# A hybrid decoder layer on eight cores: separate banks for norm sums, tile-by-tile closing, two score banks, block-diagonal q, and a decay-gate product in bf16 parts

## The chip, the cores and the metric

The program runs on the 8 cores of one Trainium2 chip. The batch has 8 sequences, and each core computes one of them alone: 2048 tokens by 1024 channels. The metric is the device time of the slowest core in microseconds (us). Each core has TensorE (PE, matrix products, with its weight loads shown as PEld), VectorE (DVE), ScalarE (ACT), GpSimd (POOL) and SyncE (SP). Here POOL and SP do hardly more than issue DMAs.

## The reference, cut to what matters

```python
h = h + 0.5 * swiglu(rmsnorm(h), wg, wu, wd)          # first feed-forward half, D_FF = 2816
u = rmsnorm(h); z = u @ w_in                           # one input projection, then split by columns
# mixer 1: latent attention, 8 heads, q and k of 64+32 (rope), v of 64, causal softmax
# mixer 2: gated linear attention, 4 heads, dk = 64, dv = 128, chunks:
log_a = log_sigmoid(a_lr @ w_a2 + b_a) / 16            # a_lr has 16 columns: the decay gate
bcum  = cumsum(log_a) inside a chunk
q_t, k_t = q * 64**-0.5 * exp(bcum), k * exp(-bcum)
o = tril(q_t k_t^T) v + q_t S                          # S: the state before the chunk
S = exp(b_last) * S + (k * exp(b_last - bcum))^T v
# mixer 3: cross-attention of 4 heads of 128 into 256 memory tokens
merged = sum of sigmoid(gate) * (o_i @ w_o_i) over the three mixers
h = h + merged @ w_out
h = h + 0.5 * swiglu(rmsnorm(h), ...)                  # second feed-forward half
out = rmsnorm(h)
```

## The kernel before, in words

**Tiles and stages.** A core's 2048 tokens are four tiles of 512, numbered 0 to 3, with channels on the partitions. A matmul is 128 by 128 weights against 512 columns of tokens unless something smaller is said. The program is written in this order: the opening (norms of tiles 0 to 2), the first feed-forward half of tiles 0, 1 and 2 together, that of tile 3 alone, the mixers of tiles 0 and 1, the second half of tile 0, the mixer of tile 2, the second half of tile 1, the mixer of tile 3, and the second half of tiles 2 and 3 together.

**A planner sets the order.** Each operation is recorded with its dependencies and a cost, and `schedule` (line 206's `dma` and the helpers record them) plays the program through once with those costs and writes down the order of each engine. The smaller the priority number, the earlier an operation is taken when several are ready. The priority is the place in the program plus `f.base`. The feed-forward halves of single tiles (tile 3's first, tile 0's and tile 1's second) get a base of a million and more, so they fill TensorE where the mixers leave it free; below they are called the filler. On the chip each engine then runs its list strictly in order and waits on semaphores.

**Banks.** The eight PSUM banks of 512 f32 columns are given out by kind, with a limit for each in `limits`: `s` for attention scores, `o` for an attention head's output, `q` and `m` for projections, `x` for cross-attention, `g` for the linear attention's output, `f` and `w` for the feed-forward halves (three or two tiles, one tile), `n` for norm sums. Banks of one kind are opened in the order in which the program asks for them: no bank of kind `f` opens before an earlier one of kind `f` has. The seven weight buffers (`ring`) work in the same manner.

**A feed-forward half** (`ffn`) goes through its 22 blocks of 128 hidden columns in five splits. In a split, `gate_up` makes 16 matmuls for a block and a tile, ScalarE a silu and VectorE a product into `aF` (or, for tile 2, into a part of `ntm`); then `down` makes one matmul for each block of the split and each of 8 output rows, and VectorE adds it to the tile's `hS`. In the last split `landed` follows each `down`: `Squares.take` lets ScalarE square the row, and a matmul with `ones` adds it up in a bank of the sums' own kind, which is asked for with the first square. From the full sum `rstd` makes the norm's factor by a logarithm and an exponential, and eight VectorE operations scale the rows to the next stage's input (`nM[0]` for the mixer of tile 0).

**A mixer** (`mixer_tile`) projects, norms, and makes keys and values for the tile; then come 8 heads of causal attention over all tiles so far (score matmul, exponential on ScalarE, matmul with the values). Between heads `fill(2)` sets units of the two other mixers: `u_v`, `u_gates`, `u_q`, `u_k`, `u_kt`, then alternately `u_chunk` (linear attention over 128 tokens) and `u_x` (a cross-attention head). The merge with its 24 gate projections and the output projection follow.

**Names in rows.** `mb,B` are score matmuls, `mb,va` those with the values, `mb,ones` and `fb,ones` norm sums, `aF,ring` and `ntm,ring` or `B,ring` feed-forward or projection matmuls by the operand that streams. `f1g`, `f2g`, `f2bg` and `wb` are weights in HBM. Lines 562, 573, 588, 595, 600, 606 and 612 are the helpers for matmuls, transposes, activations, tensor-tensor, scalar-tensor-tensor, tensor-scalar and copies. Two pairs of lines matter most:

```python
    sums = [Squares(M2, M1, "f") for _ in range(3)]
    limits = {"f": 8, "w": 4, "s": 3, "o": 1, "q": 2, "m": 6, "g": 1, "x": 2, "n": 2, ...
```

## Time and profile before

| what | value |
|---|---|
| time, median of 3 runs | 1682.48 us |
| the other runs | 1679.72 and 1876.37 us |
| the profiled execution's own time | 1687.72 us |
| its span on the slowest core (core 1) | 1686.6 us |
| spans of the eight cores | 1673.0 to 1686.6 us |
| mean granted TensorE clock of core 1 | 0.992 |
| TensorE, VectorE, ScalarE busy | 1628.0, 872.0, 730.4 us |

The median is of whole runs; the rows are of one profiled execution, whose span is 1.1 us below its own time. A matmul counts as busy for its whole pipelined length, so the busy share of TensorE overstates the work in it. The run of 1876.37 us stands far from the other two, and nothing below rests on it.

### The profile page before, as it was taken

How to read it: one execution, taken by the hardware profiler on the slowest of the kernel's cores; microseconds unless marked ns; L12 is line 12 of the kernel's file. 1: busy time of each engine (PE TensorE's matmuls, PEld its weight loads, DVE VectorE, ACT ScalarE, POOL GpSimd, SP SyncE). 2: the span in 40 equal slices, each digit the busy share in tenths (PEclk: the TensorE clock that was granted, in tenths of full speed). 3: DMA queues.
4: the chain of work that ended last, by engine and by line, in shares of the span. 5: the costliest groups of instructions: out<-in, count | busy, mean ns of one | idle time of the engine just before them, and what ended most of it. 6: DMA issues, size and time to landing. Idle time of an engine off the chain costs nothing.

```text
span 1686.6 us, 24322 instructions; the slowest of 8 cores (1673.0 to 1686.6 us)
## 1 busy us (share of the span) xinstructions
PE 1628.0 (97%) x7859; PEld 753.9 (45%) x7859; DVE 872.0 (52%) x1490; ACT 730.4 (43%) x1182; POOL 120.6 (7%) x228
## 2 busy tenths in 40 slices
PE   6999999998999999999999999999999999999997
PEld 2445444434444444444444444454444444444443
DVE  6662442435765566654565644645645464433336
ACT  5213001046872256952477862268993221210114
POOL 0102011100000000000000000000000011001000
PEclk9999999999999999999999999999999999999999
DMA  9779999898566575555998774886464455623212
GB/s 212 106 114 124 139 125 110 129 148 208 104 146 157 151 154 111 111 130 167 252 207 181 159 192 151 256 220 154 133 192 129 159 157 157 178 70 100 76 38 100
DMA packets 80425, 249.10 MB, mean 148 GB/s; under 512 B 9440, under 2 KB 13808, under 8 KB 79856
## 3 DMA queue, kind: packets, MB, share of 16 engines
q0 software_dynamic: 28864, 107.49, 38.2%
q1 hardware_dynamic: 51440, 140.06, 26.9%
q8 instruction: 68, 1.11, 0.3%
q14 instruction: 53, 0.43, 0.1%
HBM read 282.91 MB, written 54.00 MB: 200 GB/s over the span
## 4 chain that ended last, share of the span: by engine, by line
PE 89%; DMA 4%; DVE 3%; ACT 3%; issue 2%; POOL 0%; DVEq 0%; ACTq 0%; SPq 0%; POOLq 0%
PE ps_all L562 88%; DMA ring<-f1g 2%; ACT mb L588 1%; DVE hS L600 1%; DMA ring<-wb 1%; ACT ma L588 1%; ACT L588 1%; DMA ring<-f2d 1%; DVE ntm L600 0%; DMA hS<-x 0%; DVE mb L595 0%; ACT fa L588 0%; DVE aF L595 0%; DVE gU L600 0%; ACT B L611 0%
## 5 line engine op out<-in xcount | busy, mean ns | idle before, releaser
L562 PE MATMUL ps_all<-ntm,ring 128*128 128x512 bf16 x2224 | 530.5, 381 | 5.1 <-ACT ma L588 2.2
L562 PE MATMUL ps_all<-B,ring 128*128 128x512 bf16 x2016 | 450.4, 379 | 2.8 <-DVE gU L600 1.0
L562 PEld LDWEIGHTS ps_all<-ntm,ring 128*128 128x128 bf16 x2224 | 216.3, 98 | 267.1 <-issue 21.1
L588 ACT ACTIVATE fa<-ps_all 128x512 f32<-128x512 f32 x170 | 101.4, 598 | 468.9 <-PE ps_all L562 460.5
L562 PEld LDWEIGHTS ps_all<-B,ring 128*128 128x128 bf16 x2016 | 195.9, 98 | 237.7 <-issue 8.3
L562 PE MATMUL ps_all<-aF,ring 128*128 128x512 bf16 (+1 forms) x1264 | 294.3, 375 | 3.7 <-DVE hS L600 1.7
L600 DVE SCALAR_TENSOR_TENSOR hS<-ps_all,hS 128x512 f32<-128x512 f32 (+1 forms) x256 | 170.0, 672 | 99.6 <-PE ps_all L562 98.4
L595 DVE TENSOR_TENSOR aF<-fa,ps_all 128x512 bf16<-128x512 f32 x148 | 101.3, 686 | 226.0 <-PE ps_all L562 219.6
L562 PEld LDWEIGHTS ps_all<-aF,ring 128*128 128x128 bf16 x1264 | 123.4, 98 | 147.5 <-issue 10.7
L588 ACT ACTIVATE mb<-ps_all 128x512 bf16<-128x512 f32 (+1 forms) x304 | 161.5, 576 | 39.0 <-PE ps_all L562 36.0
L588 ACT ACTIVATE ma<-ps_all,hv 128x512 f32<-128x512 f32 x104 | 71.2, 687 | 183.1 <-PE ps_all L562 162.2
L588 ACT ACT_TABLE_LOAD x85 | 109.1, 1283 | 42.9 <-PE ps_all L562 27.2
L600 DVE SCALAR_TENSOR_TENSOR ma<-ma,ps_all 128x512 f32<-128x512 f32 x96 | 65.8, 687 | 113.4 <-PE ps_all L562 106.5
L562 PE MATMUL ps_all<-mb,va 128*128 128x512 bf16 (+1 forms) x320 | 108.8, 347 | 0.9 <-DVE om L595 0.5
L562 PE MATMUL ps_all<-mb,B 128*128 128x512 bf16 (+2 forms) x320 | 96.3, 348 | 4.5 <-ACT mb L588 1.7
L562 PE MATMUL ps_all<-mb,ring 128*128 128x512 bf16 (+1 forms) x416 | 93.5, 374 | 1.1 <-ACT B L611 0.9
L600 DVE SCALAR_TENSOR_TENSOR fa<-fa,ps_all 128x512 f32<-128x512 f32 x66 | 45.2, 685 | 70.8 <-ACT fa L588 66.5
L588 ACT ACTIVATE ma<-ps_all 64x512 f32<-64x512 f32 (+2 forms) x96 | 57.0, 597 | 22.3 <-PE ps_all L562 20.5
L588 ACT ACTIVATE mb<-hS 128x512 bf16<-128x512 f32 (+1 forms) x72 | 40.7, 580 | 56.4 <-DVE hS L600 49.4
L588 ACT ACTIVATE ma<-ma 128x512 f32<-128x512 f32 (+2 forms) x102 | 62.1, 619 | 5.0 <-DVE ma L976 1.0
L562 PEld LDWEIGHTS ps_all<-mb,ring 128*128 128x128 bf16 x416 | 40.5, 98 | 46.5 <-issue 6.5
L562 PE MATMUL ps_all<-mb,ones 128*128 128x512 bf16 (+1 forms) x120 | 41.6, 375 | 19.4 <-ACT mb L588 18.6
(129 smaller groups left out, 1215.1 us busy)
## 6 DMA issues: line engine op xcount, KB each, us to landing
ring<-wb SPq DMA_DIRECT2D x112, 512.0 KB, 4.4
ring<-f1g POOLq DMA_DIRECT2D x44, 512.0 KB, 10.4
ring<-f2bg POOLq DMA_DIRECT2D x44, 512.0 KB, 3.6
wb<-wm POOLq DMA_DIRECT2D x28, 512.0 KB, 14.7
ma<-spill SPq DMA_DIRECT2D x48, 256.0 KB, 5.5
ring<-wb SPq DMA_DIRECT2D x48, 256.0 KB, 3.7
ring<-f2g POOLq DMA_DIRECT2D x22, 512.0 KB, 8.6
f2bg<-ring SPq DMA_DIRECT2D x22, 512.0 KB, 5.5
```

The lines of the kernel that those rows point to most:

```text
L562: i = e.matmul(_ap(o), lhsT=_ap(l), rhs=_ap(r), start=st, stop=sp)
L588: f.add([("act", lambda e: e.activation(out=_ap(out), in_=_ap(in_), func=func, scale=_ap(scale), **kw), c_act(out, bias is not None))], ou ...
L595: f.add([(eng, lambda e: e.tensor_tensor(out=_ap(out), in0=_ap(a), in1=_ap(b), op=op), c_dve(out, rate))], outs=[out], ins=[a, b, *extra_ins])
L600: f.add([("dve", lambda e: e.scalar_tensor_tensor(out=_ap(out), in0=_ap(in0), scalar=_ap(scalar), in1=_ap(in1), op0=op0, op1=op1), c_dve(o ...
```

## The change

It has five parts.

1. **Sums' own banks.** The norm sums at the end of the two joint feed-forward stages take banks of kind `n` instead of `f`.
2. **Tile-by-tile closing of the first half.** In the last split tile 1 does its gate and up products, its downs and its norm, then tile 0, then tile 2, each followed by `close1`: before, all gate and up products came first, then all downs. Tile 1's hidden values now stand in the part of `ntm` that tile 0's mixer input takes over, tile 2's in `aF`. The reload and norm of tile 3 follow the close of tile 1 and 0, at the ordinary priority. The eight weight conversions (`wb<-wm`) of this split are issued during tile 1's products. `rope_tables` of tiles 0 and 1 get a lower priority.
3. **Two score banks** instead of three (`"s": 2`).
4. **The gated mixer.** `u_q` writes q_t of a pair of heads as a block-diagonal matrix `qz` of 128 by 1024, so one score matmul of 256 columns serves two heads (two a chunk instead of four of 128), and the state is kept as 128 by 128 for a pair instead of 128 by 256 with a mask. The copies to `ktz` and the mask `blk` go. The state's update is four matmuls with 64 weight columns and 128 streamed columns, two of which write output partitions 64 to 127. The products with the state come before those with v and take 256 columns each. `u_v` splits its weights by rows of the contraction, so it makes 8 matmuls of 512 columns where it made 16 of 256.
5. **The decay gate's product.** `a_lr @ w_a2` was a matmul in f32 with 16 rows. Now both operands are cut into three bf16 parts, laid out along 128 rows so that one bf16 matmul adds seven of the part products. The weights are cut once in `late_constants` (eight VectorE operations on 128x256), the activations once in each mixer (four small operations on 32 partitions where there was one copy).

The planner's cost of an f32 matmul is also raised, with no f32 matmul left.

```diff
@@ limits
-    limits = {"f": 8, "w": 4, "s": 3, "o": 1, "q": 2, "m": 6, "g": 1, "x": 2, "n": 2,
-              "rf": 7, "rw": 3, "rm": 4}
+    limits = {"f": 8, "w": 4, "s": 2, "o": 1, "q": 2, "m": 6, "g": 1, "x": 2, "n": 2, "rf": 7, "rw": 3, "rm": 4}
@@ late_constants
-        f.dma("sp", wa2_t, wa2_d, nbytes=16384, after=f.last_pe)
+        w32 = M2.get()
+        f.dma("sp", w32[:, 0:256], wa2_d, nbytes=131072, after=f.last_pe)
...
+        part = M1.get()
+        for i in range(3):
+            cp(part[:, 0:256], w32[:, 0:256], eng="dve")
+            if i < 2:
+                tt(w32[:, 0:256], w32[:, 0:256], part[:, 0:256], ALU.subtract)
+            if i:
+                stt(wa2_t, part[:, 0:256], vecs[:, V_SEL + i:V_SEL + i + 1], wa2_t, ALU.mult, ALU.add)
+            else:
+                ts(wa2_t, part[:, 0:256], vecs[:, V_SEL:V_SEL + 1], None, ALU.mult)
@@ mixer_tile
-        cp(ga_t, pk[0:16, :])
+        rest = M2.get()
+        cp(ga_t[0:32, :], pk[0:32, :])
+        cp(ga_t[96:128, :], pk[0:32, :])
+        tt(rest[32:64, :], pk[32:64, :], ga_t[0:32, :], ALU.subtract)
+        cp(ga_t[32:64, :], rest[32:64, :])
+        tt(ga_t[64:96, :], rest[32:64, :], ga_t[32:64, :], ALU.subtract)
@@ u_q, u_k
-                stt(st["q"].bf()[:, pr * TT:(pr + 1) * TT], p, 0.125, st["E"][pr], ALU.mult, ALU.mult)
+                for o2 in range(2):
+                    rows = slice(64 * o2, 64 * o2 + 64)
+                    stt(qz[pr][rows, o2 * TT:(o2 + 1) * TT], p[rows, :], 0.125, st["E"][pr][rows, :], ALU.mult, ALU.mult)
...
-                for o2 in range(2):
-                    o = o2 * 64
-                    cp(ktz[pr * 2 + o2][o:o + 64, :], kb[o:o + 64, pr * TT:(pr + 1) * TT], eng="dve", rate=4.0)
@@ u_v
-                mm([(p[:, v * 256:(v + 1) * 256], nM[k][:, i * 128:(i + 1) * 128], st["wv"][v][:, k, :], k == 0, k == 7)
-                    for v in range(2) for k in range(8)])
+                mm([(p, nM[k][:, i * 128:(i + 1) * 128], st["wv"][k // 4][:, k % 4, :], k == 0, k == 7) for k in range(8)])
@@ u_chunk
-            mm([(pa[:, h4 * 128:(h4 + 1) * 128], ktz[h4][:, csl], q[h4 // 2], True, True) for h4 in range(4)])
+            mm([(pa[:, pr * 256:(pr + 1) * 256].re("p (h n) -> p h n", h=2), k[pr], q[pr], True, True) for pr in range(2)])
...
-            mm([(pd[:, pr * 256:(pr + 1) * 256], kt[:, pr * 128:(pr + 1) * 128], v[:, pr * 256:(pr + 1) * 256], True, True)
-                for pr in range(2)])
+            mm([(pd[h4 % 2 * 64:h4 % 2 * 64 + 64, h4 // 2 * 128:(h4 // 2 + 1) * 128], kt[:, h4 * 64:(h4 + 1) * 64],
+                 v[:, h4 * 128:(h4 + 1) * 128], True, True) for h4 in range(4)])
...
-            for h4 in range(4):
-                o = po[:, h4 * 128:(h4 + 1) * 128]
-                g.append((o, v[:, h4 * 128:(h4 + 1) * 128], am[:, h4 * 128:(h4 + 1) * 128], True, False))
-                g.append((o, gS[n % 2][h4 // 2][:, (h4 % 2) * 128:(h4 % 2 + 1) * 128], q[h4 // 2], False, True))
+            for pr in range(2):
+                g.append((po[:, pr * 256:(pr + 1) * 256].re("p (h n) -> p h n", h=2), gS[n % 2][pr], q[pr], True, False))
+                for h4 in (2 * pr, 2 * pr + 1):
+                    hsl = slice(h4 * 128, (h4 + 1) * 128)
+                    g.append((po[:, hsl], v[:, hsl], am[:, hsl], False, h4 % 2 == 1))
...
-                stt(gU[pr], gU[pr], gp, pd[:, pr * 256:(pr + 1) * 256], ALU.mult, ALU.add)
-                stt(gS[(n + 1) % 2][pr], gU[pr], gdec[par][pr][:, i:i + 1], blk, ALU.mult, ALU.mult)
+                stt(gU[pr], gU[pr], gp, pd[:, pr * 128:(pr + 1) * 128], ALU.mult, ALU.add)
+                ts(gS[(n + 1) % 2][pr], gU[pr], gdec[par][pr][:, i:i + 1], None, ALU.mult)
@@ the first half's stage
         if j in (2, 3):
+            f.base = LATER // 2
             rope_tables(j - 2)
+            f.base = 0
...
-    sums = [Squares(M2, M1, "f") for _ in range(3)]
-    ffn(f1_d, [nB[0], nB[1], nB[2]], (0, 1, 2), "f", True, lambda i, c: sums[i].take(hslot[i][c]), side1, by_tile=(1, 0, 2),
-        opening=OPENING)
-    take_over(NTB[2], aT[2])
-    keep_rstd(1, sums[1].rstd("f"), M2)
-    spill(1, 1)
-    r = sums[0].rstd("f")
-    for c in range(8):
-        scaled(nM[0][c], hslot[0][c], V_MIX, c, r)
-    M2.put(r)
-    keep_rstd(2, sums[2].rstd("f"), M2)
-    spill(2, 2)
-    take_over(NTB[0] + NTB[1], hslot[2])
...
     f.base = LATER
-    load_x(3, 1)
-    rmsnorm(hslot[1], [vcol(V_F1 + c) for c in range(8)], D, nB[3], banks="n", wide=F2, narrow=F1)
...
+    sums = [Squares(M2, M1, "n") for _ in range(3)]
+    def close1(i):
+        r = sums[i].rstd("f")
+        if i == 0:
+            for c in range(8):
+                scaled(nM[0][c], hslot[0][c], V_MIX, c, r)
+            M2.put(r)
+            rmsnorm(hslot[1], [vcol(V_F1 + c) for c in range(8)], D, nB[3], banks="n")
+            return
+        keep_rstd(i, r, M2)
+        spill(i, i)
+        if i == 2:
+            take_over(NTB[0] + NTB[1], hslot[2])
+            return
+        take_over(NTB[2], aT[2])
+        load_x(3, 1)
+    ffn(f1_d, [nB[0], nB[1], nB[2]], (0, 1, 2), "f", True, lambda i, c: sums[i].take(hslot[i][c]), side1,
+        by_tile=(1, 0, 2), opening=OPENING, closed=close1, acts=[aT[0], aT[2], aT[1]])
@@ the last stage
-    sums_l = [Squares(M2, M1, "f") for _ in range(2)]
+    sums_l = [Squares(M2, M1, "n") for _ in range(2)]
```

**How the order moves at the first half's close.** TensorE, last split: before, the last 188 gate and up matmuls of the three tiles, then tile 1's downs with their sums.

```order
L562 MATMUL ps_all<-B,ring 128x512 x188
L562 MATMUL ps_all<-aF,ring 128x512 x4
L562 MATMUL ps_all<-mb,ones 128x512
L562 MATMUL ps_all<-aF,ring 128x512 x18
L562 MATMUL ps_all<-mb,ones 128x512
L562 MATMUL ps_all<-aF,ring 128x512 x2
L562 MATMUL ps_all<-mb,ones 128x512
L562 MATMUL ps_all<-aF,ring 128x512 x3
```

After, the same place: tile 1's last gate and up products and its downs, and further on tile 2's last products and its downs.

```order
L560 MATMUL ps_all<-B,ring 128x512 x60
L560 MATMUL ps_all<-ntm,ring 128x512 x18
L560 MATMUL ps_all<-mb,ones 128x512
L560 MATMUL ps_all<-ntm,ring 128x512 x2
L560 MATMUL ps_all<-mb,ones 128x512
L560 MATMUL ps_all<-ntm,ring 128x512 x3
...
L560 MATMUL ps_all<-B,ring 128x512 x36
L560 MATMUL ps_all<-ntm,ring 128x512 x24
L560 MATMUL ps_all<-aF,ring 128x512 x18
L560 MATMUL ps_all<-mb,ones 128x512
L560 MATMUL ps_all<-aF,ring 128x512 x2
L560 MATMUL ps_all<-mb,ones 128x512
```

The sum no longer stands between the first four downs and the rest but behind 18 of them, and 24 projection matmuls of tile 0's mixer (`ntm,ring`) stand ahead of tile 2's downs.

**In the last stage,** TensorE, where tile 2 ends. Before:

```order
L562 MATMUL ps_all<-B,ring 128x512 x60
L562 MATMUL ps_all<-aF,ring 128x512 x4
L562 MATMUL ps_all<-mb,ones 128x512
L562 MATMUL ps_all<-aF,ring 128x512 x18
L562 MATMUL ps_all<-mb,ones 128x512
L562 MATMUL ps_all<-aF,ring 128x512 x2
L562 MATMUL ps_all<-mb,ones 128x512
```

After:

```order
L560 MATMUL ps_all<-B,ring 128x512 x60
L560 MATMUL ps_all<-aF,ring 128x512 x18
L560 MATMUL ps_all<-mb,ones 128x512
L560 MATMUL ps_all<-aF,ring 128x512 x2
L560 MATMUL ps_all<-mb,ones 128x512
L560 MATMUL ps_all<-aF,ring 128x512 x3
L560 MATMUL ps_all<-mb,ones 128x512
```

The first sum moves from behind 4 downs to behind 18.

**In the attention of tile 3,** TensorE, a stretch without projections. Before:

```order
L562 MATMUL ps_all<-mb,va 128x512
L562 MATMUL ps_all<-ntm,ring 128x512 x4
L562 MATMUL ps_all<-mb,va 128x512
L562 MATMUL ps_all<-mb,B 128x512 x2
L562 MATMUL ps_all<-mb,va 128x512
L562 MATMUL ps_all<-mb,B 128x512
L562 MATMUL ps_all<-ntm,ring 128x512 x4
```

After:

```order
L560 MATMUL ps_all<-mb,va 128x512
L560 MATMUL ps_all<-aF,ring 128x512 x7
L560 MATMUL ps_all<-mb,va 128x512
L560 MATMUL ps_all<-mb,B 128x512 x2
L560 MATMUL ps_all<-mb,va 128x512
L560 MATMUL ps_all<-aF,ring 128x512 x7
L560 MATMUL ps_all<-mb,va 128x512
L560 MATMUL ps_all<-mb,B 128x512 x2
```

A score stands in both wherever a bank comes free; after, six or seven filler matmuls stand between scores where there were four. Counted over the whole list in matmuls of 512 columns, the work from the first to the last score matmul of a tile is 270, 374, 510 and 618 before and 298, 422, 562 and 778 after, of 7367 in both. From tile 3's last score to the end there are 1871 before and 1541 after.

## Rows read from the trace of the kernel before

**Rows 1.** The page: span, busy time, the chain by engine.
```profile
span 1686.6 us, 24322 instructions; the slowest of 8 cores (1673.0 to 1686.6 us)
...
PE 1628.0 (97%) x7859; PEld 753.9 (45%) x7859; DVE 872.0 (52%) x1490; ACT 730.4 (43%) x1182; POOL 120.6 (7%) x228
...
PE 89%; DMA 4%; DVE 3%; ACT 3%; issue 2%; POOL 0%; DVEq 0%; ACTq 0%; SPq 0%; POOLq 0%
```

**Rows 2.** Stages: us, length, then busy us by engine, clock, DMA.
```profile
core 1: us, PE busy (x) PEld busy (x) DVE busy (x) ACT busy (x) POOL busy (x), PEclk, DMA share, GB/s
0.00:50.00 50.00, 37.20 (x146) 14.90 (x147) 33.73 (x76) 26.05 (x41) 4.13 (x11) 0.97 0.87 193
75.00:100.00 25.00, 22.93 (x104) 9.65 (x103) 21.82 (x40) 1.85 (x3) 3.12 (x6) 1.00 0.93 120
350.00:400.00 50.00, 41.82 (x172) 16.75 (x170) 23.47 (x35) 25.82 (x43) 2.60 (x5) 0.93 0.93 189
...
400.00:1285.00 885.00, 864.28 (x4317) 406.93 (x4316) 501.59 (x892) 547.35 (x881) 39.58 (x75) 1.00 0.66 165
1285.00:1630.00 345.00, 345.00 (x1601) 156.36 (x1599) 157.13 (x232) 63.92 (x98) 33.17 (x60) 1.00 0.40 125
1630.00:1687.00 57.00, 42.36 (x222) 21.66 (x220) 28.57 (x55) 22.29 (x40) 0.00 (x0) 0.90 0.20 74
```

**Rows 3.** TensorE by shape: busy us, mean ns of one | idle before.
```profile
L562 PE MATMUL ps_all<-ntm,ring 128*128 128x512 bf16 x2224 | 530.5, 381 | 5.1 <-ACT ma L588 2.2 <-DVE hS L600 1.1 <-DVE aF L595 0.4
...
L562 PE MATMUL ps_all<-cs 16*128 16x512 f32 x16 | 9.2, 653 | 0.0
```

**Rows 4.** TensorE's timeline in a mixer: start, length, what, [idle before].
```profile
421.36 1.12 PE L562 MATMUL ps_all<-cs 16*128 16x512 f32 x2
422.41 1.04 PE L562 MATMUL ps_all<-ring,mb 128*128 128x512 bf16 x4
...
441.87 0.22 PE L562 MATMUL ps_all<-ma,gS 128*128 128x128 bf16 x1
441.93 0.22 PE L562 MATMUL ps_all<-mb,ma 128*128 128x128 bf16 x1
```

**Rows 5.** TensorE's timeline where the first half closes.
```profile
359.26 0.38 PE L562 MATMUL ps_all<-mb,ones 128*128 128x512 bf16 x1 [1.67 <-ACT mb L588]
...
385.66 0.38 PE L562 MATMUL ps_all<-mb,ones 128*128 128x512 bf16 x1 [1.86 <-ACT mb L588]
...
393.21 0.58 PE L562 MATMUL ps_all<-fb,ones 128*128 128x512 bf16 x1 [0.71 <-ACT fb L588]
```

**Rows 6.** Timeline of TensorE under the rope tables.
```profile
92.27 1.24 PE L562 MATMUL ps_all<-ntm,ring 128*128 128x512 bf16 x5 [1.10 <-DVE hS L600]
93.97 1.24 PE L562 MATMUL ps_all<-aF,ring 128*128 128x512 bf16 x5 [0.46 <-DVE hS L600]
```

**Rows 7.** TensorE's timeline where tile 2 ends its last half.
```profile
1639.15 0.38 PE L562 MATMUL ps_all<-aF,ring 128*128 128x512 bf16 x1 [0.36 <-DVE aF L595]
1641.19 0.38 PE L562 MATMUL ps_all<-mb,ones 128*128 128x512 bf16 x1 [1.67 <-ACT mb L588]
1641.40 5.73 PE L562 MATMUL ps_all<-aF,ring 128*128 128x512 bf16 x18
```

**Rows 8.** DMA issues from 355 to 400 us: KB each, us to landing.
```profile
ring<-f1g POOLq DMA_DIRECT2D x3, 512.0 KB, 12.6
```

**Rows 9.** Longest waits of TensorE, 400 to 1285 us.
```profile
PE ps_all L562 <- ACT ma L588: 3.7, 5, 1.5
```

**Rows 10.** Attention of tiles 2 and 3, columns as in rows 2.
```profile
880.00:990.00 110.00, 108.49 (x563) 51.49 (x561) 59.10 (x117) 90.53 (x151) 7.39 (x14) 0.99 0.78 180
1130.00:1260.00 130.00, 125.59 (x639) 58.58 (x638) 71.65 (x136) 114.86 (x194) 7.48 (x15) 1.00 0.60 162
```

**Rows 11.** ScalarE from 1130 to 1260 us by shape.
```profile
L588 ACT ACTIVATE mb<-ps_all 128x512 bf16<-128x512 f32 x101 | 55.9, 599 | 7.7 <-PE ps_all L562 7.1
```

**Rows 12.** VectorE, 400 to 1285 us, the linear attention's state.
```profile
L600 DVE SCALAR_TENSOR_TENSOR gS<-gU,gd,blk_s 128x256 bf16<-128x256 f32 x32 | 15.4, 482 | 2.1
```

60 lines of the change are left out of this document (32 added, 28 removed).

## The prediction

> **What bounds the kernel now.** I read the page first, then the stages, then single stretches of TensorE's timeline. The page says that TensorE is busy 1628.0 of 1686.6 us and that 89% of the chain that ended last is its matmuls [rows 1]. So two things can shorten the program: fewer or cheaper matmuls, and fewer gaps between them. Busy time overstates the matmuls. One of 512 columns lasts 381 ns in the mean [rows 3], but in the stage without a gap 1601 of them fill 345.00 us [rows 2], 0.2155 us each. A matmul of 128 columns follows its forerunner after about 0.056 to 0.06 us [rows 4], so columns set the time and an instruction costs some 2.5 ns beside them. Priced so by width, the list of the program (6987 matmuls of 512 columns, 504 of 256, 64 of 384, 288 of 128, 8 in f32) is 1598 us of pure streaming. The other 88 us of the span are gaps and stretches at a lower clock.
>
> Where they lie, from the stages [rows 2], each length less its matmuls by width: 0 to 50 us has 146 matmuls, 31.5 us of work, so 18.5 us lost; 75 to 100 has 104, 22.4 us, so 2.6 lost; 350 to 400 has 172, 37.1 us, so 12.9 lost; 1285 to 1630 loses nothing; 1630 to 1687 loses 17.5, most of it the tail behind the last matmul. The 885 us of the mixers hold what is left, about 34 us.
>
> **Part 1, the f32 product.** One f32 matmul (two records) starts at 421.36 and the next instruction at 422.41 [rows 4], 1.05 us; by the group it is 9.2 / 8 = 1.15 us [rows 3]. I take 1.10. In bf16 with 128 rows it is 0.216. Eight of them: 8 x (1.10 - 0.22) = 7.1 us off TensorE, all on its path. The other changed matmuls keep their columns: scores 4 x 128 become 2 x 256, `u_v` 16 x 256 become 8 x 512, state and output 1024 columns in fewer pieces. That is 160 instructions less in all, 0.3 to 0.4 us. Together **-7.4**. The four small operations on the activations a tile and the eight on the weights lie on VectorE and ScalarE, busy 872 and 730 of 1687 us [rows 1]; against them stand the `ktz` copies that go and the state updates at half their width, of which one took 482 ns 32 times [rows 12]. I cost these at nothing; the cover is the filler, and without it the longer chain ahead of `u_gates` would show, some 2 us a tile.
>
> **Part 2, the 64-column matmuls.** The trace has none, so I bound them. Below: two that write different halves of the partitions might overlap, 32 x 0.056 = 1.8 us saved. Above: if TensorE emptied its pipeline whenever the weight shape changes, a change would cost 381 - 216 = 165 ns [rows 3], twice in each of 16 chunks, 5.3 us. I take 0, since no row shows TensorE waiting between shapes: around the f32 matmuls, a change of rows and type, the follower starts at its price. The Trainium skill (TensorEngine Tiling (Array Packing), section Tiling Modes, under Key Properties) says that changing the tiling mode drains TensorE, which speaks for the upper end; by it the sum below would be 18 instead of 23.
>
> **Part 3, the close of the first half.** Before, the first sum matmul stands behind four downs in the order, and all later banks of its kind wait with it: TensorE stood 1.67 us at 359.26, 1.86 at 385.66, then 0.71 and more while tile 3's squares came from ScalarE [rows 5]. The clock fell too, to 1.2 GHz for some microseconds after these waits: a mean of 0.93 over the 50 us is 3.5 us of the 12.9 [rows 2]. After, 18 downs stand ahead of the first sum, other tiles' products cover the closes of tiles 1 and 0, and 24 projections of tile 0's mixer cover tile 2's; tile 3's norm comes in between. I expect a quarter of the loss to stay. Its place is weights: tile 3's blocks and the mixer's weights are wanted within some 10 to 20 us of the buffers' release (45 to 90 matmuls later in the order), and a load took 12.6 us to land here [rows 8] at a DMA share of 0.93 [rows 2]. So **-9.7**. What is moved with it: eight conversions go to the POOL queue within 14 us instead of 41, but the down weights stand ahead of them in its list; behind them stand only tile 3's first blocks. The reload of tile 3 stands on SP's queue ahead of the projection weights and waits for the spill of tile 1, which has 55 us for it.
>
> **Part 4, rope tables.** TensorE waited 1.10 and 0.46 us, and shorter, for `hS` updates queued behind rope operations on VectorE [rows 6], 2.6 us in the stage [rows 2]. In the new order at most one rope operation stands between two updates, and the second table comes in a stretch of products. **-2.3**. The weights' cutting comes shortly before; there VectorE has some 2.8 us free of every 3.5, and eight operations of at most 0.48 us are 3.8 us. If its 128 KB land late, the eight banks cover about 8 us.
>
> **Part 5, the last stage.** At 1641.19 TensorE stood 1.67 us for the first square, and the 18 downs behind it took 5.73 us where 18 x 0.216 + 0.17 = 4.1 are due [rows 7]: after the wait some of them ran at the lower of the clock's two levels, 1.2 GHz instead of 2.4 (granted clock 0.90 over the stage [rows 2]). 1.7 + 0.2 + 1.6 + a little of the 0.36 before: **-3.7**. The rest of the tail has no change.
>
> **Part 6, two score banks.** A tile's 3 banks let TensorE run ahead of ScalarE by three scores, two banks by two. ScalarE is busy 90.53 of 110 us in tile 2's attention and 114.86 of 130 in tile 3's [rows 10], and an exponential takes 599 ns [rows 11]. With two banks it will wait oftener for a score, so attention lasts longer: in the order 62 us more over four tiles (298 + 422 + 562 + 778 less 270 + 374 + 510 + 618, by 0.216). TensorE does filler meanwhile, so this costs nothing while there is filler. Behind tile 3's last score stand 1541 matmuls; merge, output projection and the last stage need about 1460 (384 + 1056 and sums), so some 80 are filler, 17 us of cover, where some 410 were before. TensorE's own waits in the mixers are many and short, the longest sum 3.7 us in five waits [rows 9]. They come from lateness of single results, and I see reasons both ways: fewer scores ahead expose it more, a less crowded ScalarE and one more bank for the others less. **0**, with -17 to +12 for the range: half of the 34 us gone, or a third more.
>
> **The sum.** -7.4 - 9.7 - 2.3 - 3.7 = -23.1 us. The profiled execution took 1687.7 us, 1.1 above its span and 5.2 above the median of the runs. A difference of this size carries over as it is: 1682.5 - 23.1 = **1659 us**.
>
> **The rivals.**
> *The mixers' waits halve.* For it: the bank that the scores give up goes to filler and projections, and many of the 34 us are waits on ScalarE, saturated at 88% in tile 3's attention [rows 10]. Against: the largest waits are for other things, such as a first product after a norm. It gives 1659 - 17 = 1642.
> *The close keeps its loss.* Late weights bring back the 9.7 us, a wait on `ring` loads in place of the wait on squares [rows 8]: 1669.
> *Each chunk drains TensorE twice.* The mechanism of part 2: 1659 + 5 = 1664. The Trainium skill's sentence quoted there is the one ground for it beside the missing row; by the trace it is neither borne out nor excluded.
> *Slower: ScalarE starves and the filler runs out.* Place: attention of tile 3. Each of its 120 exponentials waits for a score which stands behind a projection of 8 matmuls, 1.7 us, or a filler group of 4; if on the chip that is 0.7 us more each than planned, it is 84 us, of which 17 are covered, and the time is 1659 + 67 = 1726. Slower by 2% is reached from 0.57 us each. Against: ScalarE's time is planned with the same order, and the stage's plan of before (618 x 0.216 = 133 us) matches its 130.
>
> **How the numbers follow.** Forecast 0.50, halved waits 0.22, the close keeps its loss 0.15, drains 0.08, slower 0.05. The forecast's own range is 1650 to 1668. The whole range, 1641 to 1674, takes in the rivals but the last and the bounds of part 2. A measurement of this kernel tells about 2% from no change, 1649 to 1716. The halved waits fall below it, and a small part of the forecast: 0.26 faster. Slower 0.05, the same 0.69.
>
> **What would show it.** Right: 512-column bf16 matmuls `wa2s,ga` of 0.216 us, no gap over 1 us between 340 and 400 us and no lower clock there, no wait before the first `mb,ones` 45 us from the end. Part 2: the matmul behind the `64x128` ones starting more than 0.1 us late. Part 6: attention of tile 3 over 160 us long with TensorE full, and filler behind it. Wrong: gaps on `ring` loads after the close, PE idle in the last attention with ScalarE waiting for PE in every `mb<-ps_all`, or mixers whose gaps sum to something else than 34 us.

## The result, and the profile after

The changed kernel takes 1661.27 us in the median of six runs (1656.58 to 1662.19), the kernel before, on the same chip, 1681.12. The ratio is 0.988 with a 95% interval of 0.9865 to 0.9894: 20 us less, inside what counts as no change by the 2% bound. Forecast were 1659 us and 23 us less. The sum holds; several of its terms do not, as the profile shows. In some executions of any of these kernels the cores of one die show a lower clock and take longer; the ratios here and below are of the other executions.

The page of the changed kernel, to be read beside [rows 1]:

```profile
span 1659.7 us, 23972 instructions; the slowest of 8 cores (1650.2 to 1659.7 us)
...
PE 1616.8 (97%) x7691; PEld 741.1 (45%) x7691; DVE 873.4 (53%) x1501; ACT 744.1 (45%) x1195; POOL 120.2 (7%) x227
...
PE 89%; DMA 5%; DVE 2%; ACT 2%; issue 1%; SPq 0%; DVEq 0%; ACTq 0%; POOLq 0%
```

TensorE still bounds the kernel, with 168 instructions fewer. Its stages, with the columns of [rows 2]:

```profile
core 7: us, PE busy (x) PEld busy (x) DVE busy (x) ACT busy (x) POOL busy (x), PEclk, DMA share, GB/s
75.00:100.00 25.00, 25.00 (x118) 11.35 (x116) 20.32 (x33) 0.60 (x1) 3.12 (x6) 1.00 0.91 123
350.00:400.00 50.00, 46.11 (x208) 20.39 (x207) 25.98 (x40) 32.33 (x50) 1.63 (x3) 0.97 0.60 165
400.00:1262.00 862.00, 848.76 (x4100) 388.77 (x4099) 490.83 (x871) 515.55 (x824) 45.97 (x87) 0.99 0.66 171
...
1604.00:1660.00 56.00, 42.99 (x227) 22.53 (x224) 28.59 (x55) 22.17 (x40) 0.00 (x0) 0.91 0.23 76
```

75 to 100 us has no gap left (118 matmuls instead of 104). 350 to 400 holds 208 matmuls instead of 172, but a gap of 3.9 us is in it. The last stage's clock is 0.91 where it was 0.90.

To compare kernels stage by stage I add up, from the start times of TensorE's matmuls, each one's distance to the next less its price: its columns at 2.4 GHz and 2.5 ns, and 1.10 us for an f32 product, the prediction's prices. The sum of the prices is called the streaming work; it is worked out from the list of matmuls, not measured. What remains is lost to gaps and to the lower clock. Stages are cut by work done, so that the same matmuls stand in each; the numbers are medians of the six cores whose records are complete. "Attentions" is from a tile's first score to its last, "projection" the 25 us ahead of each attention, in which the key/value projection lies. The times are ratios to the kernel before on the same chip, by its 1682 us.

```
kernel                          us off  opening side close attentions projection other  ffn2 start end
before                             0     18.3   2.8  11.1     21.5       5.2      3.3     0.0     15.8
after                            -20.2   18.2   0.0   6.5      7.3      12.6      3.4     1.2     15.5
```

"Side" is the stretch with the rope tables, "other" the rest of the mixers, "ffn2 start" the stretch behind the last attention. The streaming work fell from 1598.3 to 1590.9 us, and each line and its streaming work add up to its median core's span (1676.6 and 1656.2 us) within 0.6 us. So the 20 us are: 7.4 of streaming, 2.8 at the rope tables, 4.6 in the close, 14.2 in the attentions, less 7.4 given back in the projection and about 1 behind the last attention.

**The close.** SP's queue, ScalarE and TensorE on core 7 of the changed kernel, against [rows 5]:

```profile
357.06 0.33 SPq L206 DMA_DIRECT2D hS<-x  x1
358.30 2.71 ACT L586 ACTIVATE mb<-hS 128x512 bf16<-128x512 f32 x5 [4.52 <-DMA hS<-x]
359.59 1.01 PE L560 MATMUL ps_all<-mb,ones 128*128 128x512 bf16 x2 [3.89 <-ACT mb L586]
...
359.00:363.00 4.00, 3.41 (x9) 1.26 (x10) 0.69 (x1) 3.72 (x8) 0.00 (x0) 0.57 0.89 330
```

The many short waits are one long one. It is not for weights: ScalarE waits 4.52 us for the reload of tile 3's rows, because the squares of tile 3's norm stand ahead of tile 0's last squares in its list, and TensorE's sum needs the latter. On all eight cores this is TensorE's one long wait here, 3.3 to 5.6 us. The reload is late because it waits for the spill of tile 1 out of the same rows: its last two DMAs went out from 340.16 us on and took 15.8 us to land in the median, and the reload's first DMA went out only at 352.19. Behind the wait the granted clock is 0.57 over four microseconds, most of them at 1.2 GHz.

**The projection of keys and values**, tile 1, core 7; `ga` marks the cutting of the gate's input:

```profile
613.27 0.68 DVE L593 TENSOR_TENSOR ma<-ps_all,ga 32x512 f32<-32x512 f32 x1
613.89 0.59 PE L560 MATMUL ps_all<-mb,ring 128*128 128x512 bf16 x2
614.58 0.59 ACT L609 ACTIVATE B<-ps_all 64x512 bf16<-64x512 f32 x1 [1.56 <-PE ps_all L560]
615.20 0.63 ACT L609 ACTIVATE ga<-ma 32x512 bf16<-32x512 f32 x1
615.27 0.69 DVE L610 CAST B<-ps_all 64x512 bf16<-64x512 f32 x1 [0.60 <-ACT B L609]
616.11 0.59 PE L560 MATMUL ps_all<-mb,ring 128*128 128x512 bf16 x2 [1.63 <-DVE B L610]
616.45 0.68 DVE L593 TENSOR_TENSOR ga<-ma,ga 32x512 bf16<-32x512 f32 x1
618.22 1.51 PE L560 MATMUL ps_all<-mb,ring 128*128 128x512 bf16 x4 [1.52 <-ACT B L609]
620.62 1.01 PE L560 MATMUL ps_all<-ring,mb 128*128 128x512 bf16 x2 [0.89 <-DVE B L610]
```

Two matmuls, then a wait for the copies out of their bank, and again. The same stretch of core 1 before had two waits of 0.9 us. The cutting is five operations where there was one copy (two copies, a subtraction, a copy, a subtraction), not the four that the text ahead of the prediction and its part 1 count. Nothing in the prediction speaks of this place.

**The f32 product and the state's matmuls.** By shape, the whole of core 7's mixers:

```profile
L560 PE MATMUL ps_all<-ga,wa2s 128*128 128x512 bf16 x8 | 3.1, 386 | 0.0
L560 PE MATMUL ps_all<-ma 128*64 128x128 bf16 x64 | 4.8, 231 | 0.2 <-ACT ma L586 0.2
```

and the timeline around one of each:

```profile
418.23 0.38 PE L560 MATMUL ps_all<-ga,wa2s 128*128 128x512 bf16 x1
418.44 0.81 PE L560 MATMUL ps_all<-B,ring 128*128 128x512 bf16 x3
...
694.88 0.38 PE L560 MATMUL ps_all<-mb,va 128*128 128x512 bf16 x1
695.18 0.30 PE L560 MATMUL ps_all<-ma 128*64 128x128 bf16 x4
695.42 0.39 PE L560 MATMUL ps_all<-mb,va 128*128 128x512 bf16 x1
```

The gate's product is at 0.21 us what the prediction said. From 694.88 to 695.42 are 0.54 us for one matmul of 512 columns and four of 128 columns, by width 0.216 + 4 x 0.056 = 0.44: 0.10 us over in each of 16 chunks, 1.6 us. The four together last 0.30 us from the first start to the last end. Four that follow each other at 0.056 us would last 3 x 0.056 + 0.231 = 0.40, so some of them overlap, as the run on them below shows.

**The last stage**, against [rows 7]:

```profile
1633.66 1.89 PE L560 MATMUL ps_all<-B,ring 128*128 128x512 bf16 x8
1636.93 0.60 PE L560 MATMUL ps_all<-aF,ring 128*128 128x256 bf16 x4 [1.38 <-DVE aF L593]
1638.72 0.27 PE L560 MATMUL ps_all<-mb,ones 128*128 128x256 bf16 x1 [1.19 <-ACT mb L586]
1638.83 3.58 PE L560 MATMUL ps_all<-aF,ring 128*128 128x256 bf16 x18
...
1639.00:1643.00 4.00, 4.00 (x23) 2.96 (x22) 1.75 (x5) 1.64 (x4) 0.00 (x0) 0.57 0.00 0
```

The wait on tile 2's first square is gone. Behind the waits at the turn of tile 3, 1.38 and 1.19 us, the clock is now down (0.57 in the row), on all six cores with complete records, and the end costs 15.5 us instead of 15.8. Before, of the same six only core 1, the one of [rows 7], had it down behind its wait of 1.67 us, where 18 downs took 5.73 us. On the other five, here core 7, the same wait had no fall behind it:

```profile
1633.68 0.38 PE L562 MATMUL ps_all<-mb,ones 128*128 128x512 bf16 x1 [1.67 <-ACT mb L588]
1633.89 4.04 PE L562 MATMUL ps_all<-aF,ring 128*128 128x512 bf16 x18
```

### The profile page after: what moved, and what is told of

It is laid out like the page before. It is cut to its first block, busy times and chain, and to the rows that moved or that the text cites. A ratio compares the mean times of both kernels' runs of the same rounds, so it can differ in the third digit from the quotient of the medians.

```text
span 1659.7 us, 23972 instructions; the slowest of 8 cores (1650.2 to 1659.7 us)
## 1 busy us (share of the span) xinstructions
PE 1616.8 (97%) x7691; PEld 741.1 (45%) x7691; DVE 873.4 (53%) x1501; ACT 744.1 (45%) x1195; POOL 120.2 (7%) x227
## 4 chain that ended last, share of the span: by engine, by line
PE 89%; DMA 5%; DVE 2%; ACT 2%; issue 1%; SPq 0%; DVEq 0%; ACTq 0%; POOLq 0%
PE ps_all L560 89%; DMA spill<-hS 1%; DMA ring<-f1g 1%; DMA hS<-x 1%; DMA ring<-wb 1%; ACT L586 1%; DMA rstd<-ma 1%; ACT ma L586 0%; DVE hS L598 0%; ACT mb L586 0%; DVE B L598 0%; ACT fa L586 0%; DVE aF L593 0%; DVE ma L593 0%; ACT B L609 0%
## 5 line engine op out<-in xcount | busy, mean ns | idle before, releaser
L560 PE MATMUL ps_all<-aF,ring 128*128 128x512 bf16 (+1 forms) x1264 | 301.8, 378 | 4.3 <-ACT B L609 2.1
L586 ACT ACTIVATE mb<-ps_all 128x512 bf16<-128x512 f32 (+1 forms) x304 | 165.0, 573 | 74.7 <-PE ps_all L560 71.4
L586 ACT ACTIVATE mb<-hS 128x512 bf16<-128x512 f32 (+1 forms) x80 | 44.6, 583 | 58.1 <-DVE hS L598 46.5
```

What stands on the lines that cost most here:

```text
L560: i = e.matmul(_ap(o), lhsT=_ap(l), rhs=_ap(r), start=st, stop=sp)
L586: f.add([("act", lambda e: e.activation(out=_ap(out), in_=_ap(in_), func=func, scale=_ap(scale), **kw), c_act(out, bias is not None))], ou ...
```

## The experiments

Twelve kernels. Each "us off" is the ratio to the kernel before, times 1682 us, less 1682; the ratio's 95% interval is given at each run. All twelve in the account's columns, with the two kernels for comparison:

```
kernel                          us off  opening side close attentions projection other  ffn2 start end
before                             0     18.3   2.8  11.1     21.5       5.2      3.3     0.0     15.8
before, price +1 ns              +7.9    15.7   2.8  11.2     23.1       6.6      4.1     0.4     16.3
before, two score banks         -10.3    17.0   2.8  11.8      9.5       2.5      5.5     0.8     17.5
before, parts 3 to 5             -4.4    17.7   0.0   8.5     17.0       6.3      7.9     0.0     13.7
before, mixer's parts            +3.0    17.0   4.4  11.0     19.8      11.6      6.2     0.0     16.7
after                            -20.2   18.2   0.0   6.5      7.3      12.6      3.4     1.2     15.5
after, price +1 ns              -21.4    16.7   0.0   9.9      5.3      14.7      2.4     0.8     13.7
after, price -1 ns               -4.0    17.7   2.8   6.7     13.6       7.3      6.5     8.4     14.5
after, three score banks         +0.7    17.1   0.0   8.4     18.3      13.0      7.0     5.5     13.7
after, kv banks of kind m        -3.4    17.6   0.0   8.6     11.9      10.6     10.3     6.2     14.6
after, f32 product               -7.2    16.6   0.0   8.5      8.3       5.2      8.3     6.9     15.3
after, reload planned later     -26.7    18.0   0.0   2.0      7.3      12.2      5.5     1.2     13.5
... and cutting written later   -30.3    17.7   0.1   2.0      8.9       6.5      4.2     2.7     15.3
after, 64-column probe           +5.5    17.0   0.0   8.8     12.9      13.6      6.1     1.2     14.9
```

**Three score banks again.**

```
-    limits = {"f": 8, "w": 4, "s": 2, ...
+    limits = {"f": 8, "w": 4, "s": 3, ...
```

> The changed kernel with three score banks instead of two, nothing else. My theory: in the changed kernel the two banks lowered the gaps of TensorE in the four attentions (21.5 us of loss before, 6 to 9 after) and raised them in the key/value projection just ahead of each attention, which takes its banks from the same kind (some 4 us before, 12 to 15 after, half of it low clock behind the waits). With three banks I expect the attention lengths back near 65/88/115/142 us, the attention losses back to 15 to 22 us, the loss in the 22 us ahead of the attentions back to 4 to 6 us, so 0 to 8 us more in total than the changed kernel: about 1665. Rival A, that the better attention came from the other edits (fewer instructions of the gated mixer, cheaper state updates) and not from the banks: attention losses stay at 6 to 9 us while those ahead of it fall, about 1654. Rival B, that the banks do nothing to the time: 1661, with losses as in the changed kernel.

Ratio 1.0004 (0.9987 to 1.0022). The attentions lose 18.3 us instead of 7.3, as the theory said. The projection still loses 13.0, and its two long waits, here on core 3, are the changed kernel's 1.63 and 1.52 us:

```profile
614.00 0.59 PE L560 MATMUL ps_all<-mb,ring 128*128 128x512 bf16 x2 [1.63 <-DVE B L610]
616.11 1.86 PE L560 MATMUL ps_all<-mb,ring 128*128 128x512 bf16 x4 [1.52 <-ACT B L609]
```

So the number of score banks has nothing to do with that wait, and the half of my theory that blamed it falls. The run is 21 us slower than the changed kernel, more than the 11 us of the attentions: some 10 came up elsewhere, 4 of them in one gap behind the last attention.

**The projection's banks of another kind.**

```
         for j in range(4):
-            p = bank("s")
+            p = bank("m")
             proj(wkv, j * 128, 128, ckvn, p, nk=2)
```

and the same in the loop for the values.

> The changed kernel with the eight banks a tile of the key/value up-projection taken from the filler's kind (up to six banks) instead of the scores' kind (two), nothing else. My theory: TensorE's waits for copies out of two banks just before each attention (1.63, 1.52 and 0.89 us at tile 1's in the changed kernel) go, and with them the low clock behind them (6.83 us at half clock there, 3.4 us at tile 2's): the loss in the 22 us ahead of the four attentions falls from some 12 to 15 us to 2 to 5, attention unchanged, 1651 to 1655. Rival: the waits are for VectorE and ScalarE themselves, which are busy with the norms there, so any bank waits alike; then the loss stays within 2 us and the time is 1661.

Ratio 0.998 (0.9966 to 0.9993). The projection loses 10.6 us, hardly less, so it isn't short of banks of its kind; by the account 5 us more are lost in the attentions, 7 in the rest of the mixers, 5 behind them. One of these gaps, core 3, is late weights, the next a sum that waits for VectorE:

```profile
857.44 1.19 PE L560 MATMUL ps_all<-ntm,ring 128*128 128x512 bf16 x3 [4.68 <-DMA ring<-wb]
...
1026.14 0.58 PE L560 MATMUL ps_all<-fb,ones 128*128 128x512 bf16 x1 [2.76 <-DVE fb L593]
```

A change of eight banks' kind cost 17 us against the changed kernel. Neither the theory's 1651 to 1655 us nor the rival's 1661 came out, and neither has an answer to that; it raised the question of the controls below.

**The reload planned 8 us later.**

```
-        load_x(3, 1)
+        load_x(3, 1, slack=8.0)
```

(`load_x` hands `slack` on to its DMAs, whose planned landing it delays; the instructions are the same.)

> The changed kernel with the reload of tile 3's rows told to the planner as 8 us slower than before, nothing else, so that the planner puts the squares of tile 3's norm later in ScalarE's order. My theory: the 5.6 us that are still lost in the close of the first half (350 to 400 us) come from ScalarE's squares of tile 3, which wait 4.5 us for the reload and keep the squares of tile 0's close behind them; with the later plan the waits of 1.01 us and their like on the sums and the 3.4 us at half clock go, loss 1 to 2 us, so 1657. Rival (the prediction's): the loss that stays is late weights, so gaps on ring loads stay and the close still loses some 5 us, 1661. Second rival: the squares come later than tile 3's blocks want them, and the wait moves to tile 3's first product: loss 5 us or more.

Ratio 0.9841 (0.9827 to 0.9855), 6.5 us faster than the changed kernel. The close loses 2.0 us instead of 6.5, and the stretch on core 3 keeps the full clock:

```profile
350.00:400.00 50.00, 48.12 (x224) 21.67 (x222) 29.03 (x45) 33.66 (x53) 2.16 (x4) 1.00 0.77 215
...
380.61 1.67 PE L560 MATMUL ps_all<-ntm,ring 128*128 128x512 bf16 x7 [1.88 <-DVE ntm L598]
```

The cause of the close's loss is the place of tile 3's squares in ScalarE's list. The rival, late weights, is out: no matmul waits for a `ring` load in this stretch, neither here nor in the changed kernel. The end lost 2 us less as well. The waits at its turn are still there, here on core 3, the first one shorter (1.01 us), but this time the clock stayed up behind them on five of six cores:

```profile
1628.45 0.60 PE L560 MATMUL ps_all<-aF,ring 128*128 128x256 bf16 x4 [1.01 <-DVE aF L593]
1630.25 0.27 PE L560 MATMUL ps_all<-mb,ones 128*128 128x256 bf16 x1 [1.20 <-ACT mb L586]
...
1628.00:1636.00 8.00, 5.80 (x49) 4.62 (x50) 4.13 (x10) 4.36 (x10) 0.00 (x0) 1.00 0.00 1
```

**The f32 product back.**

```
-    ga_t = T(f.sb("ga", [128, TT], BF16)[:], "ga")
-    wa2_t = T(f.sb("wa2s", [128, 256], BF16)[:], "wa2s")
+    ga_t = T(cs_h[0:16, 0:TT], "ga")
+    wa2_t = T(cs_h[0:16, TT:TT + 256], "wa2")
...
-        (the copies and subtractions that cut pk and wa2)
+        cp(ga_t, pk[0:16, :])
```

> The changed kernel with the decay gate's product back in one f32 pass over 16 rows, its three bf16 parts and the weights' cutting gone, nothing else. By the prediction's term: eight products of 1.05 to 1.15 us instead of 0.22, so 7 to 7.5 us of TensorE's work more and no other change: 1668.5. Rival: part of the f32 product's length lay beside waits of the mixers that come anyway, or the cutting of the activations costs waits of its own that now go: 2 to 4 us more only, 1664. Rival on the other side: the f32 pass delays the gates and the waits around it grow: over 1672.

Ratio 0.9957 (0.9944 to 0.997), 13 us slower than the changed kernel. The streaming work is 1597.9 us, 7.0 more, by the price of 1.10 us a product; by the start times a product takes 1.053 us here as in the kernel before, so 6.7. The projection loses 5.2 us instead of 12.6, so the cutting of the gate's input is what costs there. But the rest of the mixers and the stretch behind them lose 11 us more, so the total, beyond the rival's 1672 us, decides nothing between term and rivals.

**Two controls on the changed kernel, one on the kernel before.** No instruction is changed, only what the planner takes a matmul to cost.

```
-            cost += max(n * k / 2400.0 + 0.0025, 0.1)
+            cost += max(n * k / 2400.0 + 0.0035, 0.1)
```

> The changed kernel with every matmul priced 1 ns higher in the planner's costs, nothing else: the same instructions in another order. It tests the reading that came up with the two runs in which a small edit cost 19 to 23 us: the planner's order is sensitive, and where a result comes late on the chip is a matter of luck in each order. If that holds, the time moves by 5 to 25 us though nothing was changed, with the streaming work at 1590.9 us and other single gaps of 2 to 5 us in the close, in the merges and around the start of the second feed-forward. Rival: the order's luck is worth less than 3 us, and the 19 to 23 us were bought by the bank edits themselves: 1661 within 3.

Ratio 0.9873 (0.9856 to 0.989): as the changed kernel, though TensorE's order differs from the first attention on. The close loses 9.9 us instead of 6.5. ScalarE's order differs there: three squares of tile 0 stand ahead of tile 3's, here on core 3, and four in the changed kernel, where the wait for the reload is 5.39 us on this core.

```profile
347.48 1.82 ACT L586 ACTIVATE mb<-hS 128x512 bf16<-128x512 f32 x3 [4.08 <-DVE hS L598]
357.35 3.75 ACT L586 ACTIVATE mb<-hS 128x512 bf16<-128x512 f32 x7 [8.04 <-DMA hS<-x]
```

The spill ahead of the reload took 18.3 us to land here and 12.8 there, the reload itself 6.6 us in both. After this run I held the order's luck to be small.

> The kernel before with every matmul priced 1 ns higher in the planner's costs, nothing else. The same change of price moved the changed kernel by less than its measurement tells, though some 1340 of its lines of order changed. Is the order's luck small for the kernel before as well: 1682 within 3 us, attention losses at 18 to 22 us. Rival: the kernel before sat on an unlucky order and another one is worth 5 to 15 us, so that part of the gain of 21 us is no work of the change.

Ratio 1.0047 (1.0028 to 1.0066): 8 us slower, by 4 us of mixers and by gaps that differ between cores, so my 1682 within 3 us was wrong. So was the rival as far as one other order can tell: it is worse and not better.

The third control has 0.0015 in place of 0.0025.

> The changed kernel with every matmul priced 1 ns lower, nothing else: the second of the two controls on this side. Luck small: 1661 within 3 us. Rival: 5 us or more away, with a gap of 3 to 4 us in the merge or at the start of the second feed-forward of the kind that three of the runs with small edits show and the changed kernel does not; then those gaps are the order's, not the edits'.

Ratio 0.9976 (0.9966 to 0.9987): 16 us slower than the changed kernel, with the same instructions: the rival came true. One of its gaps, core 1, VectorE and TensorE behind the last attention:

```profile
1420.69 4.72 DVE L598 SCALAR_TENSOR_TENSOR B<-hS,vecs_s,ma 128x512 bf16<-128x512 f32 x7
...
1420.91 0.38 PE L560 MATMUL ps_all<-fb,ones 128*128 128x512 bf16 x1 [1.86 <-DVE fb L593]
1423.57 1.86 PE L560 MATMUL ps_all<-B,ring 128*128 128x512 bf16 x4 [2.27 <-DVE B L598]
...
1420.00:1428.00 8.00, 4.81 (x12) 1.70 (x13) 7.92 (x13) 4.90 (x6) 0.00 (x0) 0.64 0.01 2
```

TensorE waits 4 us in two pieces for VectorE, which is busy 7.92 of 8 us with a norm, and runs at a mean clock of 0.64 in the eight microseconds. This gap and its like (8.4 us in the column "ffn2 start") are in the runs with three score banks, with kind `m` and with the f32 product too, whose edits lie far away from it. Since it comes in the control without any edit of the instructions, I put it down to the order there too; that is argued, not shown. The order can be a part of every difference below some 15 us in this section.

**Two score banks alone, in the kernel before.**

```
-    limits = {"f": 8, "w": 4, "s": 3, ...
+    limits = {"f": 8, "w": 4, "s": 2, ...
```

> The kernel before with two score banks instead of three, nothing else (the attention part of part 6 alone). By my theory the attention losses fall from 21 us to 6 to 10 and the attentions of tiles 2 and 3 grow by some 10 and 25 us, as in the changed kernel, whatever the rest does: 10 to 15 us faster if the other stretches kept their losses, so 1668, and anything from 1660 to 1680 with another order's gaps elsewhere. Rival: the lower attention losses of the changed kernel come from its gated mixer, and stay at 20 us here: 1680.

Ratio 0.9939 (0.9921 to 0.9957), 10 us faster. The attentions lose 9.5 us instead of 21.5, and the last lasts 167 us instead of 142, with TensorE full. These are the attention of tile 3 before, after, and here, to be read by length and PE busy:

```profile
1123.00:1265.10 142.10, 137.10 (x686) 63.06 (x685) 75.36 (x143) 125.12 (x213) 8.44 (x16) 1.00 0.61 165
```
```profile
1141.80:1310.30 168.50, 168.28 (x832) 78.26 (x831) 78.97 (x150) 123.26 (x206) 13.78 (x26) 0.99 0.43 137
```
```profile
1142.50:1309.60 167.10, 165.18 (x829) 77.48 (x828) 76.58 (x144) 126.73 (x208) 13.24 (x25) 1.00 0.41 125
```

Idle in it are 5.0, 0.2 and 1.9 us; ScalarE's share falls from 88% to 73 and 76%. With the run on three banks the effect is shown from both sides, and it holds over all fourteen kernels: the attentions lose 5.3 to 13.6 us in the nine with two banks, 17.0 to 23.1 in the five with three.

Tile by tile, in us, medians again, the last column the length of tile 0's attention:

```
kernel                    tile 0  tile 1  tile 2  tile 3   tile 0 lasts
before                       5.8     5.7     2.4     7.6             65
before, two score banks      2.1     2.1     2.4     2.9             67
after                        1.4     0.7     3.5     1.6             65
after, three score banks     4.5     3.4     4.0     6.2             62
```

Only tile 3's part, 6 of the 14 us, goes with a much longer attention and a less crowded ScalarE. Tile 0's attention lasts as long as before (ScalarE busy 84%, then 81%), and of its 3.3 us of waits before, 2.8 were for VectorE. Why fewer score banks help there, no run shows.

**The prediction's parts 3 to 5 alone, in the kernel before** (the sums' banks, the close with its order of buffers, the rope tables' priority, the last stage's banks: these pieces of the change's diff and no other).

> The kernel before with parts 3 to 5 alone: the sums' own banks, the close tile by tile with its new order of buffers and side work, the rope tables' priority and the last stage's banks; three score banks, the f32 product and the old gated mixer stay. The prediction's terms give -9.7 - 2.3 - 3.7 = -15.7 us; what the changed kernel's trace shows is some 5 us off the close, 2.8 off the stage of the rope tables and nothing off the end, so 8 us less: 1673. Rival: other gaps come up in the mixers by the new order and take it back, 1680 or more.

Ratio 0.9974 (0.996 to 0.9988), 4 us faster. 2.8 us come at the rope tables, 2.6 in the close, 2.1 at the end, and 1 us more is lost in the mixers: 7 us on the median core, of which 4 are left on the slowest. Cores 0, 1 and 5 have gaps of 3.0 to 5.3 us for late `ring` loads in their mixers that the others lack.

**The mixer's parts alone, in the kernel before** (block-diagonal q, 64-column matmuls, the three bf16 parts).

> The kernel before with the mixer's parts alone: the block-diagonal q with its 64-column matmuls and the gate's product in three bf16 parts; three score banks and the joint close, the rope tables' priority and the last stage as before. Streaming work falls by 7.4 us. By the reading of the runs so far the cutting of the gate's input costs waits in the key/value projection, 6 to 9 us ahead of the attentions of tiles 1 and 2, so no gain: 1680. Rival, the prediction's part 1: its small operations cost nothing, 1675.

Ratio 1.0018 (1.0004 to 1.0032): 3 us slower, for all its 7.4 us less of streaming. The projection loses 11.6 us instead of 5.2 here too, with three score banks and the old close.

**The 64-column matmuls by themselves.** The group of four is issued five times, with one full matmul between, and the planner isn't told:

```
+            for (o, l, r, st, sp) in (group if between is None else group + 4 * [between, *group]):
...
+            between=(pd[:, 256:384], kt[:, 0:128], v[:, 0:128], True, True)
```

> The changed kernel with each chunk's group of four 64-column matmuls issued five times, with one of 128 columns by 128 into an unused part of the bank between two of them, and the planner not told, so that the order is the changed kernel's. 16 chunks x 4 x 5 = 320 matmuls of 128 columns' length more, 0.056 us each when they stream: 18 us, and 128 changes more between weights of 64 and of 128 columns. If a change costs what the changed kernel's trace shows (0.10 us for both together in a chunk): 18 + 6 = 24 us at most, 16 to 24 with some of it lying in waits that are there anyway, so 1677 to 1685. Rival, that each change drains TensorE (0.165 us): 18 + 21 = 39 us, 1700. Second rival, that matmuls on different halves of the partitions overlap: the four take less than 0.22 us in a row and the time grows by under 15 us.

Ratio 1.0033 (1.0021 to 1.0046), 26 us slower than the changed kernel. One chunk on core 3:

```profile
702.29 0.38 PE L560 MATMUL ps_all<-mb,va 128*128 128x512 bf16 x1
702.60 1.88 PE L560 MATMUL ps_all<-ma 128*64 128x128 bf16 x24
704.41 0.39 PE L560 MATMUL ps_all<-mb,va 128*128 128x512 bf16 x1
```

24 matmuls take 1.81 us, by width 1.34. One repetition (the full one and four of 64 columns) is 0.394 us, by the start times; by width 0.28. In it the four start at 0, 3, 80 and 83 ns: two that write different halves of the partitions start together. A look at 30 ns of the changed kernel's timeline, from 695.17 us on, shows two of its four begun:

```profile
695.18 0.25 PE L560 MATMUL ps_all<-ma 128*64 128x128 bf16 x2
```

By the start times of the repetitions, the first of the four starts 0.159 us after the full one, by width 0.056: 0.103 late. A pair takes 0.080 us instead of 0.112, 0.032 less. The next full one starts 0.155 us after the last pair, 0.075 late. 0.103 + 0.075 - 2 x 0.032 = 0.114 us over the columns. 16 x 4 x 0.394 = 25.2 us, and the run is 26 us slower, 2 us beyond my range. Neither rival holds alone: each change does cost, 0.08 to 0.10 us instead of 0.165, and the pairs do overlap. The Trainium skill (TensorEngine Tiling (Array Packing), section Tiling Modes, under Key Properties) has both rules, that a change of mode drains TensorE and that tiles work independently. The trace agrees as far as there is a cost at each change, less than the 0.165 us that I had put for a full drain, and an overlap of the pairs, which gives back a third of what the changes cost.

**The cutting of the gate's input written behind the projection**, with the later reload:

```
-        (the seven lines from rest = M2.get() to M2.put(rest))
...
         M1.put(*ckvn)
+        (the same seven lines)
         qh = {}
```

> The changed kernel with tile 3's reload planned 8 us later (as in the run above on the close) and the gate input's cutting in three bf16 parts written behind the key/value projection instead of ahead of it, so that its five small operations yield to the copies out of the projection's banks on VectorE and ScalarE. Theory: the waits of 1.79, 1.68, 1.19 and 0.65 us between the projection's matmuls of tile 1, which are there with two score banks and with three alike and not with the f32 product, come from these operations; the loss in the 22 us ahead of the attentions falls from 12 to some 4 us, and the time to 1648 if no other gap comes up. Rival: they come from the copies' own number (16 halves on two engines for eight banks), the loss stays and the time is 1656.

Ratio 0.982 (0.9795 to 0.9845), 30 us faster than the kernel before and 10 than the changed one; no other kernel here was faster. Of the 10, 6.5 are the later reload's. The move itself is 3.5 us, with intervals that overlap. The projection loses 6.5 us, half as much (a control without this edit came to 7.3), and the close stays at 2.0. Core 1 there, four matmuls at a time instead of two, with one wait left:

```profile
613.74 1.03 PE L560 MATMUL ps_all<-mb,ring 128*128 128x512 bf16 x4
...
615.96 1.02 PE L560 MATMUL ps_all<-mb,ring 128*128 128x512 bf16 x4
618.91 1.08 PE L560 MATMUL ps_all<-ring,mb 128*128 128x512 bf16 x4 [1.92 <-ACT B L609]
```

## Why the prediction was right, and where it was not

The time came out 2.3 us above the forecast and inside the range. By its own steps:

- **Part 1, the f32 product, -7.4.** The size was nearly right: a product takes 1.053 us before and 0.216 after, by the start times, so 6.7 us for eight, where the prediction's 1.10 makes 7.1; the rest of the term is its price of 2.5 ns an instruction. "I cost these at nothing; the cover is the filler" is the step that failed: the small operations of the cutting stand among the copies of the key/value projection, which holds TensorE. With the f32 product the projection loses 2.5 to 6.6 us (five kernels); with the three parts ahead of it 7.3 to 14.7 (eight kernels, one of them with three banks and the old close); moved behind it, 6.5. The two groups do not overlap, but the same instructions in another order took the projection from 12.6 to 7.3, so the 6.5 alone would not show it. The prediction named 2 us a tile for missing cover; it was 7.4 us in all, by the medians some 5 at tile 1 and 3 at tile 2 and nothing at tiles 0 and 3. Alone, the mixer's parts gain nothing.
- **Part 2, the 64-column matmuls, 0 of -1.8 to +5.3.** Measured +1.6, by both bounds' mechanisms at once. The argument from the f32 matmul's neighbours said nothing about this case.
- **Part 3, the close, -9.7.** Measured -4.6, in seven other kernels with this close -1.2 to -4.4, and -9.1 with the reload planned later. The mechanism was right, and with the later reload the size too, but "its place is weights" failed: the loss that stayed is ScalarE's list in order, with the squares of a late reload ahead of those that TensorE waits for. The prediction saw the reload on SP's queue, gave the spill ahead of it 55 us and asked about the queue, not about who computes on it. On core 7 the reload went out 12 us after the spill, when ScalarE's squares were due.
- **Part 4, rope tables, -2.3.** Measured -2.8, in nine of the ten kernels that have it; in the control with the lower price 2.8 us are lost later in that column's stretch.
- **Part 5, the last stage, -3.7.** Measured -0.3, and -2.1 to -2.3 in four other orders, the rest between. The first wait went. The step that failed is the clock's 1.6 us: they were read from core 1, and on the other five cores with complete records the 18 downs took 4.04 us before, so there was nothing to win. After, the clock falls behind the waits at the turn of tile 3 on all six, the first of them now 1.38 us instead of 1.01. In the other kernels these waits are 1.01 and 1.19 to 1.56 us (in the 64-column probe 1.38 and 1.19), and the clock falls behind them on none to five of the six cores, so on one core this term has one of two values, 1.7 us apart.
- **Part 6, two score banks, 0 of -17 to +12.** Measured -10 alone, -12 to -14 in the attentions. The prediction had the mechanism as its first rival, halved waits, and the length of 168 us as planned, and found "reasons both ways". For tile 3, 6 of the 14 us, the row to follow was there, ScalarE at 88% [rows 10]: spread over 26 us more, its lateness no longer reaches TensorE. For tiles 0 and 1, 9 us, the reason stays open. The starving rival had no support: TensorE is idle for 0.2 us of 168. Its argument against itself was misread: the plan's 133 us were compared with a window of 130 us, while tile 3's attention lasted 142.1, and 7.6 of the 9 us between are the loss in question. Two smaller slips: slower by 2%, 57 us over 1659 and 17 covered, wants 0.62 us a score and not 0.57; and the mixers' 34 us are 37 by the prediction's own terms (1686.6 - 1598 - 51.5), 35 on core 1 by the start times and 30 on the median core.

The account: 8.5 us of gain less than forecast in the close and at the end, 7.4 of a cost left out, 1.2 behind the last attention, against 14.2 in the attentions put at nothing (the 1.6 of part 2 are inside them) and 0.5 at the rope tables. That is 2.4 of the 2.9 us between -23.1 and -20.2: the forecast was right by cancellation. And part of the answer is the order's: the same instructions were as fast in one other order (1 us, inside the intervals) and 16 us slower in another, the kernel before 8 us slower in another. The three orders of the changed kernel mean -15 us against the one order of before, -19 against the mean of its two; the three groups of parts alone add up to -10.3 - 4.4 + 3.0 = -12.

**What stays open.** Why one order has the 4 us gap behind the last attention and another has not: I did not trace where plan and chip part. Why the attentions of tiles 0 and 1 lose less with two score banks. And why the spill ahead of the reload of tile 3 takes 12.8 us to land in one run and 18.3 in another: with ScalarE's order it sets how long the close waits.

## What to carry to other kernels

When a planner writes the order, measure a control: the same instructions with a price moved by 1 ns. Here it moved the time by up to 16 us, more than six of the nine edits did, so an edit is judged in its own stretch of the trace, work against work, and not by the total. When several small operations are put on an engine that copies results out of banks, look at which copies they stand among, whatever the engine's mean load. And when an in-order engine's operation waits for a late transfer, ask what is queued behind it: planning that transfer later was worth 6.5 us for one number.
